# Two transformer blocks on one core: the on-chip buffers are laid out on a grid of 2048 bytes

## The reference, cut to what matters

```python
# first block
h = rms_norm(x, norm_mix_pre);  z = h @ w_in_first          # 1024 -> 3232 columns
attn = rms_norm(dilated_attention(q, k, v), attn_out_gain)  # 8 heads of 64
rw = rwkv7(...)                                             # 8 heads of 64, a state carried over the tokens
x = x + rms_norm(concat([attn, rw]) @ w_out, norm_mix_post)
h = rms_norm(x, norm_ffn_pre)
x = x + rms_norm(square(relu(h @ w_ffn_up)) @ w_ffn_down, norm_ffn_post)   # 1024 -> 4096 -> 1024
# second block
h = rms_norm(x, norm_mix_2);  q, k, v, u = split(h @ w_in_2)
x = x + concat([moba_attention(q, k, v), multiscale_pool(u)]) @ w_out_2
h = rms_norm(x, norm_mlp_2)
x = x + square(relu(h @ w_up_2)) @ w_down_2
return rms_norm(x, norm_final_2)
```

## The kernel before

| buffer (operands of the large products) | address before | modulo 2048 | address after | modulo 2048 |
|---|---|---|---|---|
| `xn` | 16512 | 128 | 18432 | 0 |
| `w_raw`, `w_hi`, `w_lo` | 32896, 49280, 65664 | 128 | 34816, 51200, 67584 | 0 |
| `hsq` | 89216 | 1152 | 88064 | 0 |
| `dt_hi`, `tmp` | 93408 | 1248 | 92160 | 0 |
| `hn_odd` | 101600 | 1248 | 100352 | 0 |
| `h_hi`, `h_lo` | 105824, 122208 | 1376 | 104448, 120832 | 0 |
| `a_hi`, `a_lo` | 138592, 154976 | 1376 | 137216, 153600 | 0 |
| `y_hi`, `y_lo` | 146784, 154976 | 1376 | 145408, 153600 | 0 |
| `m_hi`, `m_lo` | 179552, 187744 | 1376 | 178176, 186368 | 0 |
| `th`, `tl` | 171360, 187744 | 1376 | 169984, 186368 | 0 |
| `D2`, `D4` | 220512, 224608 | 1376 | 219136, 223232 | 0 |

## Time and profile before

### The profile page before, as it was taken

The page is one execution under the profiler, slowest core; times in us unless marked ns, Lnnn a source line. Parts: engine busy times, 40 slices in busy tenths (PEclk is TensorE's granted clock), DMA queues, the critical chain, the costliest instruction groups (busy, mean ns, idle before and its releaser), DMA issues.

```text
span 1238.2 us, 26863 instructions
## 1 busy us (share of the span) xinstructions
PE 1205.6 (97%) x11189; PEld 1103.8 (89%) x11189; DVE 871.9 (70%) x1153; ACT 664.1 (54%) x1154; POOL 420.7 (34%) x345
## 2 busy tenths in 40 slices
PE   8999999998999999999999999999999999999998
PEld 6777797787898999999999997866889999999997
DVE  6678646566468689887895666435576897888953
ACT  4555536557355447456475544544454474564652
POOL 7022226333005247267261141000052472672500
PEclk9999999999999999999999999999999999999999
DMA  6223300002343233333344232122232333333331
GB/s 203 69 68 102 102 2 2 4 3 81 131 150 121 69 103 104 102 103 113 92 171 154 77 107 82 35 69 86 69 101 70 103 103 103 103 107 99 103 120 69
DMA packets 103231, 113.10 MB, mean 91 GB/s; under 512 B 2099, under 2 KB 97381, under 8 KB 103110
## 3 DMA queue, kind: packets, MB, share of 16 engines
q1 hardware_dynamic: 103030, 111.12, 28.4%
q0 software_dynamic: 80, 0.26, 0.1%
HBM read 107.18 MB, written 4.19 MB: 90 GB/s over the span
## 4 chain that ended last, share of the span: by engine, by line
PE 84%; DVE 7%; ACT 4%; issue 2%; DVEq 1%; ACTq 1%; POOL 1%; POOLq 0%
PE ps L627 8%; PE ps L628 7%; PE ps L629 7%; PE ps L718 5%; PE ps L719 5%; PE ps L720 5%; PE ps L591 4%; PE ps L593 4%; PE ps L592 4%; PE ps L773 3%; PE ps L775 3%; PE ps L774 3%; PE ps L678 1%; PE ps L680 1%; PE ps L679 1%
## 5 line engine op out<-in xcount | busy, mean ns | idle before, releaser
L627 PE MATMUL ps<-w_hi,a_hi 128*128 128x256 f32 x640 | 179.5, 280 | 0.3
L628 PE MATMUL ps<-w_lo,a_hi 128*128 128x256 f32 x640 | 178.8, 279 | 0.0
L629 PE MATMUL ps<-w_hi,a_lo 128*128 128x256 f32 x640 | 178.5, 279 | 0.0
L2065 DVE TENSOR_TENSOR w_lo<-w_raw,w_hi 128x2048 fp32r<-128x2048 f32 (+1 forms) x43 | 98.1, 2282 | 45.5 <-ACT w_hi L1398 45.2
L627 PEld LDWEIGHTS ps<-w_hi,a_hi 128*128 128x128 f32 x640 | 120.2, 188 | 1.2 <-DVE w_lo L2194 1.1
L628 PEld LDWEIGHTS ps<-w_lo,a_hi 128*128 128x128 f32 x640 | 120.3, 188 | 0.1
L629 PEld LDWEIGHTS ps<-w_hi,a_lo 128*128 128x128 f32 x640 | 120.3, 188 | 0.0
L718 PE MATMUL ps<-th,w_hi 128*128 128x256 f32 x384 | 109.2, 284 | 1.6 <-ACT tmp L1496 1.6
L720 PE MATMUL ps<-th,w_lo 128*128 128x256 f32 x384 | 107.9, 281 | 0.0
L719 PE MATMUL ps<-tl,w_hi 128*128 128x256 f32 x384 | 107.8, 281 | 0.0
L2173 DVE TENSOR_TENSOR w_lo<-w_raw,w_hi 128x1024 fp32r<-128x1024 f32 (+1 forms) x72 | 100.0, 1403 | 4.4 <-ACT w_hi L1471 4.4
(11 more groups left out here) (467 smaller groups left out, 3885.2 us busy)
## 6 DMA issues: line engine op xcount, KB each, us to landing
w_raw<-w_ffn_up_dram SPq DMA_DIRECT2D x16, 1024.0 KB, 5.7
w_raw<-w_ffn_down_dram SPq DMA_DIRECT2D x16, 1024.0 KB, 5.3
w_raw<-w_up_dram SPq DMA_DIRECT2D x16, 1024.0 KB, 5.8
w_raw<-w_down_dram SPq DMA_DIRECT2D x16, 1024.0 KB, 5.2
w_raw<-w_in_first_dram SPq DMA_DIRECT2D x12, 1024.0 KB, 5.4
w_raw<-w_out_dram SPq DMA_DIRECT2D x8, 1024.0 KB, 5.2
xn<-x_dram SPq DMA_DIRECT2D x8, 512.0 KB, 6.0
w_raw<-w_in_dram SPq DMA_DIRECT2D x4, 1024.0 KB, 6.3
```

The costliest lines, as they stand in the source:

```text
L627: mm(o, hi[:, hb + k, tok], whi, start=first and own and k == ks[0], stop=False, skip_group_check=True)
L628: mm(o, hi[:, hb + k, tok], wlo, start=False, stop=False, skip_group_check=True)
L629: m = mm(o, lo[:, hb + k, tok], whi, start=False, stop=last and k == ks[-1], skip_group_check=True)
L2065: v.tensor_tensor(w_lo[:, g % 2, :, 0:n], w_raw[:, g % 2, :, 0:n], w_hi[:, g % 2, :, 0:n].bitcast(F32), ALU.subtract).then_inc(sm["w_lo_re ...
```

## The change

Nothing of the computation, the loops, the semaphores or the transfers changes: the lists of instructions of all engines, with their waits, are the same in the same order, and only the addresses differ. The small vectors `ssq`, `sd`, `mhalf`, `eps`, `qkscale` and `pre` and the constants `page`, `par` and `ident` move in front of the first large buffer, with 160 bytes of padding (`to_grid`), so that the first large buffer begins at 18432, which is 9 times 2048. The constants `ones`, `ones64` and `centre` move behind the region of the feed-forward (`ffn_region`, 90112 bytes, only reserves it). All large buffers in between then start at a multiple of 2048. The parts of the areas for the attention and the recurrence that stand behind a small buffer stay off the grid (`uT`, `Yt`, `Fb`, `Sc`, `ktb` and others).

```diff
+        ssq = sb("ssq", [P, TT, 4])
+        sd = sb("sd", [P, 2 * TT])
+        mhalf = sb("mhalf", [P, H])
+        eps = sb("eps", [P, 3])
+        qkscale = sb("qkscale", [P, 2])
+        pre = sb("pre", [P, TT])
+        sb("to_grid", [P, 40])
+        page = sb("page", [P, P])
+        par = sb("par", [P, P])
+        ident = sb("ident", [P, P])
         with ExitStack() as s:
             dt_f32_1 = held(s)("dt_f32_1", [P, 4, KH, GW])
...
         w_lo = sb("w_lo", [P, 2, KT, GW], F32R)
-        page = sb("page", [P, P])
-        par = sb("par", [P, P])
-        ident = sb("ident", [P, P])
-        ones = sb("ones", [P, P])
-        ones64 = sb("ones64", [P, P])
-        centre = sb("centre", [P, P])
         rstd = sb("rstd", [P, S])
         delta = sb("delta", [P, S])
         hsq = sb("hsq", [P, 2, S])
-        eps = sb("eps", [P, 3])
-        qkscale = sb("qkscale", [P, 2])
-        mhalf = sb("mhalf", [P, H])
...
         hn_odd = sb("hn_odd", [P, D])
-        ssq = sb("ssq", [P, TT, 4])
-        pre = sb("pre", [P, TT])
-        sd = sb("sd", [P, 2 * TT])
...
             xl_lo = r("xl_lo", [P, 2, S], F32R)
+        sb("ffn_region", [P, 5 * KT * S + 2 * KH * GW])
+        ones = sb("ones", [P, P])
+        ones64 = sb("ones64", [P, P])
+        centre = sb("centre", [P, P])
```

## The result

| | before | after |
|---|---|---|
| median | 1240.43 us (6 runs, 1238.96 to 1242.26) | 1246.45 us (6 runs, 1245.57 to 1248.02) |
| ratio, with its 95% interval | | 1.0047 (1.0037 to 1.0056) |
| the profiled execution, its span | 1239.91, 1238.2 | 1245.57, 1243.8 |
| PE busy | 1205.6 | 1213.0 |

The forecast was 1241.5 us and no change. The time lies 0.45 us above the upper end of the range, and nearest to the first price of rival C (1245.5). The forecast and its rivals were counted from 1241.91, the median of three runs; six runs of the kernel before give 1240.43. As a change, +6.0 us, the result lies nearest to the second price of rival C, +6.3 us.

A forecast was written before the change was run, and what follows sets the result against it. TensorE matmuls, a number times a pace, were taken to bound the kernel. All terms were 0 except -0.4 us for slower row-product stretches: 1239.91 became 1239.5, plus 2.0 to the median, 1241.5 us; range 1236.2 to 1246.0 us.

The forecast's parts named there:

- rival C: Operands meeting at the same offset slow row products: first price +3.6 us (1245.5 us), second +6.3 us (1248.2); chance 0.21.
- Reads that cross a boundary: In the large matmuls, reads no longer crossing 2048-byte boundaries would be worth 0 us, bounds +-0.3 us.
- Rival B: Matmul excess above the clock comes from crossing 1024-byte boundaries: down 79 us to 1163; chance 0.06 for sizes above 10 us.
- The 32 bytes past a multiple of 64: Token operands losing their 32-byte offset from multiples of 64 would change matmul time by 0 us; bounds -4.6 and +6.3 us.
- the sign of a wrong forecast: Any of the three matmul shapes changing its pace by more than 0.6 ns over most of its matmuls.
- the pair of the earlier trace: Products of 512 columns with exchanged operand roles, 233.4 and 233.3 ns, taken to show that the 32-byte offset costs 0.
- Rival A: Column products of 256 pay for the 32-byte offset: -4.6 us, perhaps -0.9 more, 1236.4 to 1237.3 us; chance 0.31.
- The slower stretches of row products: 720 feed-forward row products at 117.8 instead of 116.6 ns, 0.9 us; half taken as gained, -0.4 us.
- ACT, DVE, GpSimd, transfers at 0: Operations on the other engines would change by 0 us, bounds -1.4 and 0; transfers by 0 us.
- The base of the forecast: The median of the runs was put 2.0 us above the profiled execution's 1239.91 us.

The follow-up runs named there:

- e7: The kernel before with 32 bytes of padding behind `w_lo`, nothing else; 1246.68 us against 1241.77.
- e4: The kernel after with all large buffers moved 32 bytes on, their distances kept; 1246.82 us against 1239.7 of before.
- e1: The kernel after with all large buffers moved 128 bytes on, their distances kept; 1246.59 us against 1239.7 of before.
- e11: The kernel after with pads of 192 bytes before the token buffers, 128 before `a_hi`, 128 before `th`; 1237.31 us, ratio 0.9976 to before.
- e13: Like e11, but with 64 in place of 192 bytes behind `w_lo`; 1235.7 us, ratio 0.9965 to before.
- e2: The kernel after with everything behind the weights moved 32 bytes on, weights kept on the grid; 1242.85 us against 1239.7 of before.
- e14: The kernel after with `w_lo` alone moved 64 bytes on; 1243.82 us against 1240.0 of before.
- e15: The kernel after with `w_hi` alone moved 64 bytes on, two fillers lengthened to match; 1246.15 us against 1240.52 of before.
- e8: The kernel before with 96 bytes of padding behind `w_lo`, one run; 1234.74 us against 1241.77.
- e12: The kernel before with 96 bytes of padding behind `w_lo`, five runs; median 1233.41 us against 1240.0, ratio 0.9948.

## Why the prediction was wrong

- **Reads that cross a boundary, taken at 0: right, and more.** After and e7 have the same paces within 0.2 ns, with no read of the table's buffers across a boundary of 2048 bytes in the one and, as in the kernel before, many in the other. Rival B, the much faster case, has nothing for it; in the products of 512 a part of the excess does go on the grid (20.0 to 13.4 ns), but it goes in e7 as well, where no large buffer lies on the grid.
- **"The 32 bytes past a multiple of 64 ... I take 0 from this": the step that failed.** The offset itself is worth 0 (e4), as I took it; but the step named the other side of it in the same breath, the row products, "which now get moving and stationary operands with the same offset, as no product has before", and put 0 to +6.3 us on it. The runs showed +8.8 us for the row products, +1.3 for the column products and -4.9 for the products of 512, because the distance between the two operands modulo 256 bytes sets the pace (e1, e4, e7; e11 and e13 for one operand alone). All three shapes moved by more than the 0.6 ns that was named as the sign of a wrong forecast (2.9, 1.6 and 5.3 ns). Two things went wrong. I gave the pair of the earlier trace rows as the nearest row that shows 0; they sit at s = +32 and -32, and in the products of 512 these two paces happen to be equal (233.2 both). A pair that differs in nothing that matters is no evidence that nothing matters. And I took 118.4 ns, the slowest pace then seen, as the bound for a relation between operands that the trace did not contain. A bound by the slowest row holds only if the new case is of the same kind as some row; here the true value, 120.0, was outside.
- **Rival C was the mechanism, at too small a price.** Slower row products because both operands begin at the same place: shown, by e7 and by its mirror cases. Its price of +3.6 or +6.3 us lacked three terms: 120.0 in place of 117.8 or 118.4 ns (+10.6 us of steady time), the column products, which also meet at distance 0 and lose 4.2 us, and the products of 512, which gain 5.6. That the change, +6.0 us, comes so near to its second price of +6.3 is luck: the price was for the row products alone at 118.4 ns, and it was met because losses of 14.8 us of steady time were set off by gains in the products of 512 and by shorter waits. I had argued against it that "the stationary block already moves in steps of 512 bytes and the steady pace of the earlier trace rows doesn't follow it"; a step of 512 is two periods of 256, so that row could not speak against it.
- **Rival A** (column products quicker without the offset): wrong in sign, 118.4 to 120.0 ns. The 1.7 ns between row and column products before were real, but they are the two signs of one distance of 32, as e2 shows by exchanging them.
- **The slower stretches of row products, -0.4 us:** there are none of two kinds on the grid; nearly all row products (369 of 396 blocks of nine) go at 120.0. So there was nothing left to halve; both kinds got slower. The count of 720 was too low besides: in the kernel before 103 of 395 blocks go at 118 ns or more, a quarter of the row products and not a fifth. At a distance of 64 two paces are back, further apart.
- **ACT, DVE, GpSimd, transfers at 0:** right, by the rows above.
- **The base of the forecast:** the 2.0 us from the profiled execution to the median came from three runs; with six runs they are 0.5. The forecast, meant as no change, so stood 1.1 us above the kernel before as measured.
- **What was left out:** that waits shrink when TensorE slows. By steady paces alone the change would have cost 9.2 us; the span grew by 5.6.

What stays open: the mechanism inside the chip. That the load of one block and the stream of another read the same memory together is the picture that led to the distance, and the dependence on s agrees with it; but e14 and e15 did not show which load a stream meets, and no kernel without weight loads was run, so that the load is the cause is argued and not shown. Nor is it known what gives a stretch at a distance of 64 the quick or the slow pace.

## What to carry to other kernels

When TensorE is the bound and each matmul loads a new block, read the start-to-start pace in the timeline and compare it with the columns at the granted clock; the excess (here 6.7 to 13.3 ns of 256 columns) depends on where the two operands lie relative to each other modulo 256 bytes, and aligning both to the same grid chose nearly the slowest distance for 256 columns. Try a few pads of 32 to 192 bytes between the weight and the activation buffers: 96 bytes gave 0.52% here. Take several runs of each, since one layout can run at two paces, and don't add up paces alone, since about half of a gain can go into waits. And before a relation is priced by the slowest row of a trace, ask whether any row has that relation at all.

## What the runs showed of the hardware that was not expected

- The pace of these matmuls (float32r operands, 128x128 blocks, one load per matmul) depends on the distance of the two operands' starts modulo 256 bytes and on no absolute start that was tried: 120.0 ns for 256 columns at distance 0 wherever the pair lies (after, e1, e4, e7), 113.4 or 117.8 at 64 either way. On the same lines and the same stream it follows the staying operand's buffer alone (e11, e13: 229.1 and 233.0 to 233.2 ns).
- The distance has a sign: 118.3 ns at +32 against 116.7 or 117.8 at -32, about 118 at +96 against 120.0 at -96, and for 512 columns 233.3 at +64 against 229.5 at -64. And 256 and 512 columns rank the distances differently: 0 is the quickest for 512 (226.7 ns) and among the slowest for 256; 64 is the quickest for 256.
- Some paces are whole numbers of cycles at 2.4 GHz: 256 + 16 (113.3), 256 + 32 (120.0), 512 + 32 (226.7). Others, as 117.8, are not.
- With one layout a stretch holds one of two paces for over 100 matmuls (113.4 or 117.8 ns), and two executions of one kernel differ in it on the same instructions (e8, e12). That this is why e12's runs spread over 5.8 us, where those of after spread over 2.5, is not shown: e11 and e13 mix the two paces as well, and their runs spread over 1.8 and 0.9 us.
